# A third pair of slabs by Strassen's products in the first mixer of a two-layer MoE trunk

## The reference

```python
def _mixer_ab(h, w_in, a_qn, a_kn, b_qn, b_kn, b_sink, w_out):
    proj = jnp.einsum('bsd,de->bse', h, w_in)          # 1024 -> 2304
    qa, ka, va, qb, kb, vb = jnp.split(proj, AB_SPLITS, axis=-1)
    qa, ka = _rmsnorm(qa, a_qn), _rmsnorm(ka, a_kn)    # per head of 64
    qb, kb = _rmsnorm(qb, b_qn), _rmsnorm(kb, b_kn)
    oa = _dilated_mixture(qa, ka, va, slopes[0::2])
    ob, _ = _banded_attention(qb, kb, vb, B_WINDOW, B_BLOCK, 1.0, slopes[1::2], sink=b_sink)
    o = jnp.concatenate([oa, ob], axis=-1)
    return jnp.einsum('bse,ed->bsd', o, w_out)
# each layer: x += mixer(rmsnorm(x)); x += moe(rmsnorm(x)), 32 experts of 256, top 2 in one of 4 groups
```

## Time and profile before

| | |
|---|---|
| median of 3 runs | 618.3 us (618.0 to 618.88) |
| profiled execution | 618.75 us, its span 616.7 us |
| mean granted clock of TensorE | 0.981 |
| busy: TensorE, VectorE, ScalarE | 565.0, 199.0, 136.6 us |
| DMA | 233.39 MB, mean 378 GB/s |

### The profile page before, as it was taken

One profiled execution on the slowest core, in us unless ns is written; L12 is line 12 of the kernel. 1 busy time (PEld: TensorE's weight loads), 2 busy tenths in 40 slices (PEclk: granted clock), 3 DMA queues, 4 the chain that ended last, 5 costly groups with the idle time before them and its releaser, 6 DMA issues.

```text
span 616.7 us, 9572 instructions
## 1 busy us (share of the span) xinstructions
PE 565.0 (92%) x3884; PEld 373.5 (61%) x3884; DVE 199.0 (32%) x613; ACT 136.6 (22%) x353; POOL 9.9 (2%) x25
## 2 busy tenths in 40 slices
PE   8999999998999939998999999999899996997897
PEld 7887777783555333555468876779355435444454
DVE  3847555153111101111045687416212011011101
ACT  3144445341001101001031366524100110110101
POOL 1200000000000000000001000000000000000000
PEclk9999999999999969999999999999999997999899
DMA  8999786589999999999999994539999999999996
GB/s 316 424 421 420 282 361 218 204 329 409 430 430 425 442 425 424 433 435 409 421 415 421 421 421 206 207 122 354 373 427 431 428 435 424 430 426 432 413 421 271
DMA packets 24245, 233.39 MB, mean 378 GB/s; under 512 B 2688, under 2 KB 3328, under 8 KB 6656
## 3 DMA queue, kind: packets, MB, share of 16 engines
q1 hardware_dynamic: 22176, 227.14, 88.6%
q10 hardware_dynamic: 2016, 5.52, 2.5%
HBM read 231.60 MB, written 1.05 MB: 377 GB/s over the span
## 4 chain that ended last, share of the span: by engine, by line
PE 70%; DMA 20%; issue 4%; DVE 3%; ACT 3%; ACTq 0%; DVEq 0%
DMA ring<-in_moe_w 18%; PE banks L1118 13%; PE banks L851 10%; PE banks L984 8%; PE banks L1092 7%; PE banks L1188 6%; PE banks L1204 6%; PE banks L866 3%; PE banks L944 2%; PE banks L823 2%; PE banks L961 2%; PE banks L972 2%; DMA desk<-in_bias 1%; PE banks L1103 1%; PE banks L995 1%
## 5 line engine op out<-in xcount | busy, mean ns | idle before, releaser
L1118 PE MATMUL banks<-ring,desk 128*32 128x512 f32 x768 | 90.1, 608 | 5.4 <-DMA ring<-in_moe_w 5.3
L1448 ACT ACTIVATE desk<-banks 128x256 f32<-128x256 f32 x16 | 6.1, 383 | 272.7 <-PE banks L1118 272.7
L851 PE MATMUL banks<-ring,hT 128*128 128x256 f32 x288 | 65.3, 381 | 0.0
L1092 PE MATMUL banks<-desk,hT 128*128 128x128 f32 x384 | 49.5, 291 | 15.4 <-issue 15.4
L984 PE MATMUL banks<-heads,ring 128*128 128x256 f32 x256 | 61.9, 387 | 0.1
L1092 PEld LDWEIGHTS banks<-desk,hT 128*128 128x128 f32 x384 | 49.0, 208 | 16.7 <-issue 16.2
L851 PEld LDWEIGHTS banks<-ring,hT 128*128 128x128 f32 x288 | 53.7, 190 | 8.6 <-issue 1.8
L1118 PEld LDWEIGHTS banks<-ring,desk 128*32 128x32 f32 x768 | 23.7, 112 | 57.0 <-issue 51.9
L984 PEld LDWEIGHTS banks<-heads,ring 128*128 128x128 f32 x256 | 46.4, 190 | 12.6 <-issue 6.9
L1204 PE MATMUL banks<-desk 128*128 128x256 f32 x224 | 52.1, 386 | 0.0
L1204 PEld LDWEIGHTS banks<-desk 128*128 128x128 f32 x224 | 41.4, 190 | 16.8 <-issue 11.7
(11 more groups left out here) (201 smaller groups left out, 649.1 us busy)
## 6 DMA issues: line engine op xcount, KB each, us to landing
ring<-in_moe_w SPq DMA_DIRECT2D x66, 1024.0 KB, 26.7
ring<-in_moe_w SPq DMA_DIRECT2D x16, 4096.0 KB, 27.5
ring<-in_moe_w SPq DMA_DIRECT2D x17, 2048.0 KB, 12.7
ring<-in_ab_w_in SPq DMA_DIRECT2D x8, 1024.0 KB, 16.8
shared<-in_moe_w SPq DMA_DIRECT2D x8, 1024.0 KB, 7.6
shared<-in_moe_w SPq DMA_DIRECT2D x2, 4096.0 KB, 27.5
shared<-in_moe_w SPq DMA_DIRECT2D x3, 2048.0 KB, 11.3
ring<-in_c_w_in SPq DMA_DIRECT2D x5, 1024.0 KB, 20.3
```

What stands on the lines that cost most here:

```text
L851: ins = pe.matmul(bank2(SLAB_BANK[layer][s], NT)[:, t, :], hT[:, c, t * P:(t + 1) * P], w[:, c, :], start=(c == 0 and t == 0), stop=(c == ...
L1092: ins = pe.matmul(bank(2 + half)[:, c * P:(c + 1) * P], tokens[:, t, half * HALF + c * P:half * HALF + (c + 1) * P], onehot_of(rd, to)[:, ...
L1118: ins = pe.matmul(bank(0)[j * SLOTS:(j + 1) * SLOTS, :], gathered_of(rd, place)[:, c, j * SLOTS:(j + 1) * SLOTS], w[:, j, :], start=(c == ...
```

## The change

`PAIRED` becomes ((3, 4), (5, 6), (7, 8)): slab 5, values, and slab 8 are no longer plain. The sums of weights get a second set of buffers, used in turn, so `SUMS_AT` falls from 16 to 15 and one buffer fewer of the ring is free from the start. The four sums of weights of a pair are separate entries (3, 1, 2, then 4) at their own places. Slabs 7 and 8 are normed as one group; slab 6 alone. A pair may now have a values slab (5), whose tiles ScalarE takes with the scale of the token. The residual's first two banks wait for tiles of the last pair. `ORDER_0` is written anew from the first product of the second pair on.

```diff
-PAIRED = ((3, 4), (6, 7))
-SUMS_AT = 16
+PAIRED = ((3, 4), (5, 6), (7, 8))
+SUMS_AT = 15
...
-        NORM = [[(0, 1), (3, 4), (6, 7), (8,)], [(0,), (2,), (3,), (4,), (5,)]]
+        NORM = [[(0, 1), (3, 4), (6,), (7, 8)], [(0,), (2,), (3,), (4,), (5,)]]
...
-            + each("prob_values", 4) + each("normalise", 5) + rows((2, 0), (2, 1))
+            + each("prob_values", 4) + each("normalise", 5) + rows((0, 4), (1, 4))
...
                 elif j == 2:
                     product_done(act, pair, 2)
-                    room_for(first)
-                    A.activation(unnormed(0, first)[:, 0, :], x[:, 0, :], ACT.Copy).then_inc(s_c11, 1)
+                    kind, _, col, _ = SLAB_PLAN[0][first]
+                    if kind == "values":
+                        A.activation(values[0][:, 0, col:col + 4 * HD], x[:, 0, :], ACT.Copy, scale=rstd[:, 0:1])\
+                            .then_inc(s_c11, 1)
+                        return
+                    if kind != "shared2":
+                        room_for(first)
+                    A.activation(tile_of(first, 0), x[:, 0, :], ACT.Copy).then_inc(s_c11, 1)
...
-                if cp < 2:
+                if layer == 0 and cp == 0:
+                    act.wait_ge(s_c11, len(PAIRED))
+                elif layer == 0 and cp == 1:
+                    act.wait_ge(s_tiles, 3 * len(PAIRED))
+                elif cp < 2:
...
-            def add_weights(pair):
+            def add_weights(pair, i):
...
+                if i == 3:
+                    for s in PAIRED[pair]:
+                        unit_arrived(dve, s)
+                    if pair >= 2:
+                        pair_done(dve, pair - 2)
+                else:
+                    dve.wait_ge(s_wsum, 4 * pair + (3, 1, 2, 4).index(i))
```

More of the change, by code:

```diff
@@ L564, in products, with sums @@
             return [("product", pair, j) for j in which]
+        def sums(pair, *which):
+            return [("weights", pair, i) for i in which]
         def rows(*pieces):
@@ L573, in hybrid_moe_kernel @@
             each("sums", 0) + each("rstd", 0) + each("tokens", 0) + parts(1, 0, 1, 2, 3)
-            + each("norm", 0) + each("weights", 0) + parts(2, 0, 1, 2, 3)
+            + each("norm", 0) + sums(0, 3, 1, 2, 4) + parts(2, 0, 1, 2, 3)
             + each("turn", 0) + products(0, 1) + each("turn", 1) + products(0, 5)
-            + each("scores", 0) + products(0, 6, 7) + each("normalise", 0) + products(0, 2, 3)
-            + each("turn_prob", 0) + each("scores", 1) + products(0, 4) + parts(5, 0)
@@ L588, in hybrid_moe_kernel @@
-            + each("turn_prob", 5) + each("scores", 6) + rows((0, 4), (1, 4))
-            + each("prob_values", 5) + each("normalise", 6) + rows((2, 2), (2, 3))
-            + each("turn_prob", 6) + each("scores", 7) + rows((2, 4), (0, 5), (1, 5)) + each("prob_values", 6)
-            + each("normalise", 7) + rows((2, 5), (0, 6), (1, 6), (2, 6)))
+            + each("scores", 0) + products(0, 6, 7) + each("normalise", 0) + sums(1, 3, 1, 2) + products(0, 2, 3)
+            + each("turn_prob", 0) + each("scores", 1) + products(0, 4) + products(1, 1)
@@ new lines, in hybrid_moe_kernel @@
+            + each("prob_values", 0) + each("normalise", 1) + products(1, 5) + each("norm", 1) + products(1, 6)
+            + sums(1, 4) + each("turn_prob", 1) + products(1, 7) + sums(2, 3, 1, 2) + each("turn", 3) + products(1, 2)
+            + each("turn", 4) + each("prob_values", 1) + products(1, 3) + each("scores", 2) + products(1, 4)
+            + products(2, 1) + each("normalise", 2) + products(2, 5) + each("turn_prob", 2) + each("norm", 2)
+            + each("scores", 3) + products(2, 6) + each("prob_values", 2) + products(2, 7) + sums(2, 4)
@@ new lines, in hybrid_moe_kernel @@
+            + each("normalise", 3) + each("turn", 6) + products(2, 2) + each("residual", 0) + each("turn_prob", 3)
+            + products(2, 3) + each("prob_values", 3) + products(2, 4) + each("residual", 1) + each("norm", 3)
+            + rows((0, 0), (0, 1), (0, 2), (0, 3), (1, 0), (1, 1)) + each("turn", 7) + rows((1, 2))
+            + each("turn", 8) + each("residual", 2) + each("scores", 4) + rows((1, 3), (2, 0), (2, 1), (2, 2))
+            + each("normalise", 4) + each("turn_prob", 4) + each("scores", 5) + rows((2, 3))
@@ L593, in hybrid_moe_kernel @@
+            + each("prob_values", 4) + each("normalise", 5) + rows((0, 4), (1, 4))
+            + each("turn_prob", 5) + each("scores", 6) + rows((2, 4))
+            + each("prob_values", 5) + each("normalise", 6) + rows((0, 5), (1, 5))
+            + each("turn_prob", 6) + each("scores", 7) + rows((2, 5)) + each("prob_values", 6)
+            + each("normalise", 7) + rows((0, 6), (1, 6), (2, 6)))
         ORDER_1 = (
@@ L839, in slab @@
                     b = SLAB_BANK[layer][s]
-                    pair = [i for i, (first, _) in enumerate(PAIRED) if layer == 0 and b in SLAB_BANK[0][first:s]]
-                    if pair:
-                        pe.wait_ge(s_c11, pair[-1] + 1)
-                    elif b in SLAB_BANK[layer][:s]:
+                    if b in SLAB_BANK[layer][:s]:
                         slab_taken(pe, layer, max(k for k in range(s) if SLAB_BANK[layer][k] == b))
@@ L860, in product @@
                 wa, wb = slab_weights(0, first), slab_weights(0, second)
+                t2, t3, t4 = [weight_sums[:, pair % 2, i, :, :] for i in range(3)]
                 low_half, high_half = slice(0, NC // 2), slice(NC // 2, NC)
@@ L877, in product @@
                 elif j == 5:
-                    slab_taken(pe, 0, first - 1 if pair else 1)
+                    if pair:
+                        pe.wait_ge(s_tiles, 3 * pair)
+                    else:
+                        slab_taken(pe, 0, 1)
                     pe.wait_ge(s_tsum, 1)
@@ L1590, in add_product @@
                     dve.wait_ge(s_u, pair + 1)
+                    if pair and SLAB_PLAN[0][PAIRED[pair - 1][0]][0] == "values":
+                        dve.wait_ge(s_val, values_before(0, PAIRED[pair - 1][0]) + 1)
                     V.tensor_tensor(widened, kept, y[:, 1, :], ALU.add).then_inc(s_v, 1)
```

54 lines of the change are left out of this document (24 added, 30 removed).

## The result

The changed kernel takes **632.4 us** (median of 5 runs, 632.15 to 632.79) against 618.53 (618.0 to 619.19) for the kernel before, measured beside it: a ratio of 1.0224 with a 95% interval of 1.021 to 1.0238. The forecast was 624.8 us, range 621.2 to 628.5. Its sign was right. It was 7.6 us too low, and the time lies outside the range. The profiled execution has a span of 630.2 us (before: 616.7) and a mean granted clock of 0.970 (before: 0.981).

What follows compares the result with a forecast made beforehand. TensorE, nearly gapless, bounds the first mixer; the experts' weight stream behind it passes on any delay. Terms -1.7 + 0.6 + 0.4 + 0.9 + 6.3 (copies and table) = +6.5 us on 618.3 give 624.8 us, range 621.2 to 628.5.

Steps and rivals of the forecast that it cites:

- The saving, -1.7: First mixer, TensorE: slabs 5 to 8 as two pairs take fourteen quarters instead of fifteen, saving 1.7 us.
- First new wait, +0.6: Turning of pair 3's probabilities: TensorE waits for VectorE's normalisation, queued behind additions and a sum of weights; net +0.6 us.
- Normed together, +0.4, and pair 4, +0.9: First mixer: TensorE waits for slabs 7 and 8 normed as one group, +0.4 us; then for pair 4's probabilities, +0.9 us.
- The copies, three waits of 2.0: Output-projection pieces (0, 4), (0, 5), (0, 6) each wait 2.0 us for ScalarE's copy of attention outputs, queued behind exponentials.
- The table, +0.8: Pair 5's bias table, issued at 93.1 into queued weight loads, lands at 97.9, 0.8 us late, between 0 and 4.1.
- rival (b): Pair 5's bias table takes the 8.1 us of a busy stream: 628.1 us, chance 0.11.
- The clock, 0: First mixer, TensorE: gaps of two microseconds don't bring back the half rate; no term in the sum.
- rival (f): The waits throw TensorE's clock to its lower level, 5 us of work: 630 us, chance 0.01.
- No slack behind it: Behind the first mixer: the stream of weights makes no slack, so the +6.5 us reaches the end.
- Rival (c): The experts take up half of the delay, because loads start relatively sooner to TensorE's need: 621.5 us, chance 0.07.
- (d): The copies don't bind, ScalarE reaching each within 0.3 us of the value step: 618.9 us, chance 0.04.
- (e): Faster: all new waits are covered and only the saved product is left: 616.6 us, chance 0.05.

Runs made afterwards that it cites:

- experiment 7: Changed kernel with VectorE's last sum of weights of the third pair behind attention pair 3's normalisation instead of ahead of it: 631.87 us, ratio 1.0205.
- experiment 9: Kernel of 6 with slabs 7 and 8 normed apart and pair 4's scores ahead of slab 8's turning: 617.61 us, ratio 0.9983.
- 6: Changed kernel with three weight loads each held for one table and the first mixer's order rewritten from pair 3's scores on: 620.04 us, ratio 1.0014.
- experiment 8: Changed kernel with only the weight loads spread, three of them each held for the position table of pair 5, 6 or 7: 627.8 us, ratio 1.014.
- experiment 2: Changed kernel with one weight load, and all behind it, held until pair 5's position table has landed: 630.75 us, ratio 1.02.
- 4: Kernel before with output-projection pieces (0, 4), (1, 4), (0, 5), (1, 5) moved right behind the value steps, swapped with four others: 620.93 us, ratio 1.0045.
- Experiment 3: Changed kernel with idle matmuls filling TensorE's waits behind the value steps of pairs 4, 5 and 6, nothing reordered: 629.07 us, ratio 1.017.

## Why the prediction was right in sign and wrong in size

By its own steps, in the traces of before and after (13.5 us found, 6.5 predicted):

- **The saving, -1.7.** It held, with the next step. From the first plain slab to the end of the third pair the changed kernel takes 67.02 us (14.23 to 81.25) and the kernel before 67.74 for the same work and a quarter of a slab more (14.01 to 81.75), though the changed one has a turning of 0.43 us more in it. With 1.73 us saved (the length of a quarter in the earlier trace rows; no run takes it by itself), 0.43 + 0.58 were added.
- **First new wait, +0.6.** The wait itself was there, idle 0.77 us and then a turning of 1.38, until 76.6 as worked out, because VectorE's second normalisation stands at 75.42, behind a sum of weights, where it stood at 74.19:

```profile
73.36 1.22 DVE L1606 TENSOR_TENSOR ring<-ring 128x1024 f32<-128x1024 f32 x1
...
75.42 0.62 DVE L1743 TENSOR_SCALAR shared<-shared,rowinv 128x256 f32<-128x256 f32 x2
```

 Undoing its cause alone brought 1.1 us (experiment 7). That is the wait with nothing taken off; set against the waits that the kernel before had in the same stretch, what is left is the 0.58 us above, and the forecast was 0.6. This step held.
- **Normed together, +0.4, and pair 4, +0.9.** The waits are 0.76 and 0.52. With the saving, these terms put pair 5's scores at 96.0; they stand at 96.45, an error of 0.45 us for four steps, and half of it, 0.22, is the offset. In the rewritten order, norming apart with the scores one place sooner brought about 2 us (experiment 9 against 6).
- **The copies, three waits of 2.0.** They measured 1.93 and 1.93, and 1.93 for each of the three where no table was late (experiment 8). The pieces start behind the copy 5.14 us after the scores wherever the table is in time (110.02 to 115.16, 119.63 to 124.77), as read from the earlier trace rows. This step was the mechanism of the loss and it held.
- **The table, +0.8: a failed term.** "so I take 97.9" was wrong. It landed 7.7 us after issue, about 101.2, and the copy of pair 4's output came 8.9 us behind the scores instead of 5.95: **+2.9 us** more. The bounds held it (4.1 at 8.1 us), and rival (b) had that price alone. I took the middle since the loads would have drained at 97.3 and the table with them. But all transfers, the table's included, had drained only at about 99.2 (246 GB/s in the window 98 to 100, 6 in the next), and the table landed two more microseconds later. In the DMA view of this stretch the queue that carries the table (q10) shows no packet until 96.5 us, 3 us behind the issue, while the weights' (q1) fills the engines; with the loads held (experiment 8) the table's first packets move 0.7 to 1.2 us behind its issue. The rows that I had, 7.6 and 8.1 us, were the measured ones for this situation, and the reasoning that took me below them was not.
- **The clock, 0: the largest failed term.** The sum had it at nothing, and rival (f) at 0.01. "by these rows gaps of two microseconds don't" rested on the window 148 to 150 us, and misread it: TensorE is idle there twice, for 1.03 and 0.47 us with work between, not once for two.

```profile
148.87 0.44 PE L1154 MATMUL banks<-small,desk 128*128 128x128 f32 x2 [1.03 <-DVE desk L1853]
149.14 0.38 PE L1156 MATMUL banks<-small,desk 128*128 128x128 f32 x2
150.00 3.64 PE L1188 MATMUL banks<-ring,desk 128*32 128x512 f32 x32 [0.47 <-ACT desk L1450]
```

 In these runs ten gaps of 1.93 or 1.94 us stood behind a value step (2 after, 2 in experiment 2, 1 in 4, 2 in 7, 3 in 8), and the clock fell behind five. It fell with each of the four of 3.1 us and more ahead of a piece or a turning (5.68, 5.33, 3.10, 5.49). A fall behind a gap of 1.93 costs 1.6 to 1.7 us, behind a longer one 1.7 to 2.6; in the changed kernel from the copy to the next scores it took 4.69 and 4.47 us where 2.75 were counted, **+1.9 and +1.7**. Experiment 3, worth 3.3 us, shows the same: a chance of a half behind each of three waits was missing from the sum. Rival (f) also had its price from a stretch where most of the low clock lay in idle time, so its 5 us was too high. The Trainium skill (TensorE: Matmul & The Clock Gate, Part 1) says that an idle TensorE goes back to its half rate; the traces agree where it fell, at 0.50, and in five of the ten short gaps it did not fall.
- **No slack behind it.** Confirmed: +13.47 us at pair 7, +13.4 at layer 1, +13.5 at the end. Rival (c) falls, (d) and (e) with it.

The errors add up: 0.45 up to pair 5's scores, 2.9 for the table, 3.6 for the clock, 7.0 in all, and 13.5 - 6.5 is 7.0. The rest of the 7.6 us against the forecast is that it was counted from a median of 618.3, while the trace before is of an execution of 618.75. So two steps failed, the table's landing and the clock; the saving and the smaller waits, taken together, came as worked out to within a quarter of a microsecond once the offset is taken off, and so did each copy.

What stays open: why a gap of 1.93 us throws the clock in one place and not in another. In experiment 7 it was the one at the third copy, in the changed kernel and experiment 8 the one at the second. Nor do the runs show why executions of experiments 6 and 8 lie up to 3 us apart; a gap that falls on either side would do that, but only one execution of each was traced.

## What to carry over

Before an instruction is placed right behind its producer, look at what stands ahead of the copy that lies between them on the other engine's in-order queue: here ScalarE's copy ended 5.1 us behind the next scores wherever the table was in time, and a place 2 us too early costs that wait each time it recurs. In this kernel a new wait of about 2 us on TensorE is to be priced as the wait plus an even chance of 1.7 us at the lower clock behind it. Take the size of a small transfer issued into a backlog from rows with a backlog (7.5 to 8.3 us for the tables of pairs 5 and 6 here, 3.3 to 4.2 without), not from when the backlog should be gone. And a product saved is worth something only if the order around it is written anew: the same saving gave +13.9 us as first ordered and -0.9 us with the loads spread, the pieces placed behind their copies, and the slabs normed apart.

## What the hardware showed that I had not expected

- Behind gaps of 1.93 us, TensorE's clock fell to 0.50 in five of ten cases; the fall shows in the rows as two pieces of 1.99 us taking 2.75 to 3.06, and 3.60 to 3.78 behind the waits of 3.10 us and more. Filling the gaps with 40 idle matmuls won 3.3 us.
- The 512 KB table of pair 5 or 6 took 7.5 to 8.3 us whenever it was issued into queued 1 MB loads, and 3.3 to 3.6 us when the loads were held. Nearly half of the excess stands ahead of its first packet: 3 us from issue instead of about 1. Holding one load back only moved the collision from the table of pair 5 to that of pair 6 (8.3 us); it took one hold for each table to end it, which was worth 4.6 us in the changed kernel and 3.8 in the new order, in each case with a fall of the clock that went too.
- In the changed kernel the transfers were idle (6 GB/s, 100 to 102 us) while the table was still awaited.
